# Output projection and normalisation in token chunks of 512, 512 and 128

## The reference, cut to what matters

```python
h = rmsnorm(x, norm_g) * (1.0 + scale) + shift          # scale, shift, gate: one set per group
y = merge_branches(g, (o_na, o_f, o_d), zs, w_branch[l], w_out[l])   # last step: y @ w_out
xs = xs + gate * y
...
y_sample = rmsnorm(xs, final_g)                          # after the last layer; y_prompt likewise
```

## Time and profile before

| What | Value |
|---|---|
| Time, median of 3 runs (lowest to highest) | 2940.79 us (2940.73 to 2941.08) |
| The profiled execution's own time | 2940.5 us |
| Its span, first to last instruction | 2938.6 us |
| TensorE busy | 2877.4 us, 98% of the span |
| VectorE, ScalarE, GpSimd busy | 45%, 37%, 21% |
| Matmuls of the output stage (L823) in the chain that ended last | 6% of the span |
| Granted TensorE clock, mean | 0.996 |

### The profile page before, as it was taken

How to read it: one execution, slowest core, us unless ns; L and a number is a source line. 1 busy time by engine, 2 the same in 40 slices (tenths; PEclk the granted TensorE clock), 3 DMA queues, 4 the chain that set the end, 5 groups by cost and what they waited for, 6 DMA issues and landing times.

```text
span 2938.6 us, 44082 instructions
## 1 busy us (share of the span) xinstructions
PE 2877.4 (98%) x18396; PEld 2756.4 (94%) x18396; DVE 1330.6 (45%) x2291; ACT 1076.5 (37%) x1947; POOL 614.0 (21%) x312
## 2 busy tenths in 40 slices
PE   6999999999999999999999999999999999999998
PEld 5999999999999999999999999999999989899997
DVE  4343443123557575446344434421146567554543
ACT  4333333221444544422343333323133444443231
POOL 0221221122221212122431221211221121211242
PEclk9999999999999999999999999999999999999999
DMA  5332224102111102254421121220211111215532
GB/s 224 102 110 82 102 90 137 67 15 78 42 47 47 48 32 94 80 203 141 133 79 65 66 82 39 94 83 22 70 41 45 44 48 47 78 51 183 165 110 94
DMA packets 84278, 248.55 MB, mean 85 GB/s; under 512 B 9201, under 2 KB 30193, under 8 KB 83057
## 3 DMA queue, kind: packets, MB, share of 16 engines
q1 hardware_dynamic: 84080, 245.74, 24.5%
HBM read 191.71 MB, written 54.00 MB: 84 GB/s over the span
## 4 chain that ended last, share of the span: by engine, by line
PE 89%; DVE 5%; ACT 2%; DMA 2%; issue 1%; SPq 1%; DVEq 0%; POOL 0%; POOLq 0%; ACTq 0%
PE ps L730 44%; PE ps L713 18%; PE ps L823 6%; PE ps L769 6%; PE ps L900 3%; PE ps L1041 3%; PE ps L1032 2%; PE ps L961 2%; PE ps L888 2%; PE ps L943 1%; DVE e L1839 1%; DVE stat L1822 1%; ACT e L1435 1%; DMA wmod<-w_mod 1%; DVE aTl L1846 1%
## 5 line engine op out<-in xcount | busy, mean ns | idle before, releaser
L730 PE MATMUL ps<-hhi,whi 128*128 128x384 f32 x2640 | 916.3, 347 | 5.7 <-DVE obuf L1854 3.3
L730 PE MATMUL ps<-hhi,wlo 128*128 128x384 f32 x2640 | 886.3, 336 | 0.0
L730 PE MATMUL ps<-hlo,whi 128*128 128x384 f32 x2640 | 884.1, 335 | 0.0
L1956 POOL TENSOR_TENSOR wlo<-wraw,whi 128x1024 fp32r<-128x1024 f32 (+1 forms) x188 | 415.8, 2212 | 2063.6 <-ACT whi L1127 2063.5
L730 PEld LDWEIGHTS ps<-hhi,whi 128*128 128x128 f32 x2640 | 500.0, 189 | 24.1 <-issue 7.3
L730 PEld LDWEIGHTS ps<-hlo,whi 128*128 128x128 f32 x2640 | 497.1, 188 | 0.9
L730 PEld LDWEIGHTS ps<-hhi,wlo 128*128 128x128 f32 x2640 | 495.9, 188 | 0.0
L1127 ACT ACTIVATE whi<-wraw 128x1024 fp32r<-128x1024 f32 (+1 forms) x188 | 174.5, 928 | 229.9 <-PE ps L713 209.3
L1444 ACT ACTIVATE aTh<-ps 128x512 fp32r<-128x512 f32 (+1 forms) x200 | 96.5, 482 | 278.4 <-PE ps L1032 278.4
L1691 DVE TENSOR_TENSOR ptl<-ps,pth 128x512 fp32r<-128x512 f32 (+1 forms) x144 | 82.1, 611 | 246.8 <-ACT pth L1301 246.6
L1822 DVE TENSOR_REDUCE stat<-ps 128x1 f32<-128x1152 f32 x144 | 176.5, 1231 | 16.9 <-PE ps L769 16.0
(11 more groups left out here) (199 smaller groups left out, 4835.8 us busy)
## 6 DMA issues: line engine op xcount, KB each, us to landing
wraw<-w_in SPq DMA_DIRECT2D x128, 512.0 KB, 4.2
gates_dram<-gst SPq DMA_DIRECT2D x48, 576.0 KB, 3.0
gth<-gates_dram SPq DMA_DIRECT2D x48, 576.0 KB, 4.9
mraw<-w_mod SPq DMA_DIRECT2D x32, 512.0 KB, 3.8
wraw<-w_branch SPq DMA_DIRECT2D x48, 256.0 KB, 2.8
bias<-rpb SPq DMA_DIRECT2D x8, 1280.0 KB, 6.0
outs_dram<-obuf SPq DMA_DIRECT2D x16, 576.0 KB, 3.9
oraw<-outs_dram SPq DMA_DIRECT2D x16, 576.0 KB, 3.8
```

The source lines that it names most:

```text
L730: x = mm(ps[:, bank, 0:CH], a[:, s % 2, k, :], b[:, k, n * CH:(n + 1) * CH], start=(k == 0 and a is whi and b is hhi), stop=(k == KT - 1 a ...
L1956: g_.tensor_tensor(lo[:, 0:kt, :], wraw[:, n % 2, 0:kt, :], hi[:, 0:kt, :].bitcast(F32), ALU.subtract).then_inc(S.w_lo, 1)
```

## The change

The output stage and the normalisation behind it run over chunks of 512, 512 and 128 tokens, so that the last chunk is just the context tokens and each instruction has one modulation. The two-part instructions of chunk 2 go. The buffers `xold`, `csqs` and `csq` grow to 512 columns; `crstd` and `ctn` also, and move over a part of the gate buffer `gth`, which is free then. The residual kept in DRAM and the output are split into two latent chunks and one context part. All counts of units, semaphores and the order on each engine stay. The units of the next layer's input projection keep chunks of 384.

```diff
+OC = ((0, 512), (512, TL), (TL, T))
...
-    xold = pl("xold", [P, 4, CH])
-    csqs = pl("csqs", [P, CH])
-    csq = pl("csq", [P, 2, CH])
-    crstd = pl("crstd", [P, CH])
-    ctn = pl("ctn", [P, 2, CH])
+    xold = pl("xold", [P, 4, 512])
+    csqs = pl("csqs", [P, 512])
+    csq = pl("csq", [P, 2, 512])
...
+    pl = Place(arena0 + KT * TB + 4 * KT * TILE_B)
+    crstd = pl("crstd", [P, 512])
+    ctn = pl("ctn", [P, 2, 512])
...
-    def parts(n):
-        if n < NC - 1:
-            return ((0, CH, 0),)
-        return (0, TL - n * CH, 0), (TL - n * CH, CH, 1)
+    def token_part(n):
+        return slice(OC[n][0], OC[n][1]), OC[n][1] - OC[n][0], int(n == NC - 1)
...
             def sum_squares(l, n):
                 pe.wait_ge(S.sq_added, (l * NC + n + 1) * (KT - 1))
-                mm(ps[:, 5, 0:CH], ones[:], csqs[:], start=True, stop=True).then_inc(S.ss_done, 1)
+                w = token_part(n)[1]
+                mm(ps[:, 5, 0:w], ones[:], csqs[:, 0:w], start=True, stop=True).then_inc(S.ss_done, 1)
...
-                hi, lo = halves(s)
+                (hi, lo), (cols, w, _) = halves(s), token_part(n)
...
-                        x = mm(ps[:, bank, 0:CH], a[:, k, :], b[:, k, n * CH:(n + 1) * CH],
+                        x = mm(ps[:, bank, 0:w], a[:, k, :], b[:, k, cols],
...
-                        for a, b, j in parts(n):
-                            x = v.scalar_tensor_tensor(out=xT[:, m, n * CH + a:n * CH + b], in0=ps[:, 6 + m % 2, a:b],
-                                                       scalar=mul_g[:, m, j:j + 1], in1=xold[:, i % 4, a:b],
-                                                       op0=ALU.mult, op1=ALU.add)
-                        x.then_inc(S.out_evac, 1)
+                        cols, w, j = token_part(n)
+                        v.scalar_tensor_tensor(out=xT[:, m, cols], in0=ps[:, 6 + m % 2, 0:w], scalar=mul_g[:, m, j:j + 1],
+                                               in1=xold[:, i % 4, 0:w], op0=ALU.mult, op1=ALU.add).then_inc(S.out_evac, 1)
```

More of the change, by code:

```diff
@@ L638, in old_load @@
                         sp.wait_ge(S.out_evac, l * NC * KT + i - 3)
-                    sp.dma_start(xold[:, i % 4, :], xs_dram[n, m] if l else x_in[m, :, n * CH:(n + 1) * CH]).then_inc(x_load[i % 4], 16)
+                    cols, w, ctx = token_part(n)
+                    kept = xs_ctx[m] if ctx else xs_dram[n, m]
+                    sp.dma_start(xold[:, i % 4, 0:w], kept if l else x_in[m, :, cols]).then_inc(x_load[i % 4], 16)
                 def result(n, half):
@@ L685, in _ @@
                         sp.wait_ge(S.out_evac, out_no(l, n, m) + 1)
-                        sp.dma_start(xs_dram[n].rearrange("k p t -> p k t"),
-                                     xT[:, :, n * CH:(n + 1) * CH]).then_inc(S.store, 16)
+                        cols, w, ctx = token_part(n)
+                        sp.dma_start((xs_ctx if ctx else xs_dram[n]).rearrange("k p t -> p k t"), xT[:, :, cols]).then_inc(S.store, 16)
                     if l + 1 == DEPTH and n and m in (5, KT - 1):
@@ L1209, in chunk_squares @@
                     act.wait_ge(S.sq_added, (KT - 1) * u + m - 2)
-                fn(csq[:, m % 2, :] if m else csqs[:], xT[:, m, n * CH:(n + 1) * CH], ACT.Square).then_inc(S.sq_ready, 1)
+                cols, w, _ = token_part(n)
+                fn(csq[:, m % 2, 0:w] if m else csqs[:, 0:w], xT[:, m, cols], ACT.Square).then_inc(S.sq_ready, 1)
             def chunk_norms(l, n):
@@ L1217, in chunk_norms @@
                     act.wait_ge(*((S.y_ready, n * KT) if l else (S.h_ready, KT + n * KT)))
-                fn(crstd[:], ps[:, 5, 0:CH], ACT.Ln, bias=eps[:, 0:1], scale=1.0 / D)
+                w = token_part(n)[1]
+                fn(crstd[:, 0:w], ps[:, 5, 0:w], ACT.Ln, bias=eps[:, 0:1], scale=1.0 / D)
                 act.drain()
-                fn(crstd[:], crstd[:], ACT.Exp, scale=-0.5).then_inc(S.rstd_ready, 1)
+                fn(crstd[:, 0:w], crstd[:, 0:w], ACT.Exp, scale=-0.5).then_inc(S.rstd_ready, 1)
             def chunk_high(n, m):
@@ L1559, in chunk_scaled @@
                 i = n * KT + m
[L1560 to L1563, removed]
+                cols, w, j = token_part(n)
+                v.scalar_tensor_tensor(out=ctn[:, i % 2, 0:w], in0=xT[:, m, cols], scalar=mul_a[:, m, j:j + 1],
+                                       in1=crstd[:, 0:w], op0=ALU.mult, op1=ALU.mult).then_inc(S.t_ready, 1)
             def chunk_input(n, m):
@@ L1574, in chunk_input @@
                 dve.wait_ge(S.hi_ready, KT + i + 1)
[L1575 to L1579, removed]
+                cols, w, j = token_part(n)
+                v.scalar_tensor_tensor(out=hlo[:, m, cols], in0=ctn[:, i % 2, 0:w], scalar=modr[:, m, j:j + 1],
+                                       in1=hhi[:, m, cols].bitcast(F32), op0=ALU.add, op1=ALU.subtract).then_inc(S.h_ready, 1)
             def chunk_result(n, m):
@@ L1585, in chunk_result @@
                     dve.wait_ge(S.rstd_ready, 2 + NC + n)
-                x = xT[:, m, n * CH:(n + 1) * CH]
-                v.scalar_tensor_tensor(out=x, in0=x, scalar=fgcol[:, m:m + 1], in1=crstd[:], op0=ALU.mult, op1=ALU.mult
+                cols, w, _ = token_part(n)
+                x = xT[:, m, cols]
+                v.scalar_tensor_tensor(out=x, in0=x, scalar=fgcol[:, m:m + 1], in1=crstd[:, 0:w], op0=ALU.mult, op1=ALU.mult
                                        ).then_inc(S.y_ready, 1)
@@ L1964, in add_squares @@
                 pool.wait_ge(S.sq_ready, KT + out_no(l, n, m) + 1)
-                g_.tensor_tensor(csqs[:], csqs[:], csq[:, m % 2, :], ALU.add).then_inc(S.sq_added, 1)
+                w = token_part(n)[1]
+                g_.tensor_tensor(csqs[:, 0:w], csqs[:, 0:w], csq[:, m % 2, 0:w], ALU.add).then_inc(S.sq_added, 1)
             g_.memset(ident[:], 0.0)
@@ L2136 @@
                "new_diff_v": lambda a: heads_rows(a, 1)}
-    y = np.ascontiguousarray(r["y_out"].transpose(0, 3, 1, 2).reshape(T, D))
-    return y[None, TL:], grid_rows(y[:TL]), *(as_rows[n](r[n]) for n in as_rows)
+    y = np.ascontiguousarray(r["y_out"].transpose(0, 3, 1, 2).reshape(TL, D))
+    return np.ascontiguousarray(r["y_ctx"].reshape(D, TC).T)[None], grid_rows(y), *(as_rows[n](r[n]) for n in as_rows)
```

16 lines of the change are left out of this document (9 added, 7 removed).

## The result

The changed kernel takes 2968.3 us (median of three executions: 2968.21, 2985.09, 2968.30) against 2940.79: **1.0116 times the time before, with an interval of 1.0095 to 1.0136**. The direction was forecast, the size was not: 2968.3 lies 11 us above the forecast of 2957 and 2.3 above the end of the range. The profiled execution took 2968.21 us, with a span of 2966.3 and a mean granted clock of 0.992.

The account below looks back on a forecast made before the run. TensorE, busy for 98% of the span, was taken to bound the kernel. Terms 15.9 + 3.1 + 3.7 − 1.4 − 5.0 = +16.3 us on the profiled 2940.5 gave 2956.8, 2957 against the median; range 2947 to 2966.

Parts of the forecast that it names:

- The matmuls: Output matmuls, both layers: a set of 512, 512, 128 takes 568 ns, 41.5 more than three of 384; +15.9 us.
- rival 2: 128-column matmuls run at their columns' pace, 65 ns, with weight loads hidden: 2943 us, not slower; chance 0.11.
- pairs in two halves of the array: Attention-score pairs of 512 columns, 0.2275 us a pair, taken as the pace of 512-column output matmuls: 228 ns.
- the bound by proportion, 234: 512-column output matmuls: growth proportional to columns from 175.5 ns at 384 gives 234 ns; 4.6 us more.
- The sum of squares: Last chunk's unit 0, both layers: TensorE waits 1.55 us for chunk 1's sum of squares; +3.1 us.
- The input chain: Layer 0's last chunk: making the next layer's inputs on VectorE and ScalarE outlasts the matmuls, TensorE waits; +3.7 us.
- the 2.45 us for each of the five tiles behind it: Layer 0's input chain: five tiles with an add before them take some 2.45 us each, 2.8 before.
- The forecast's lower bound: Layer 0's input chain: wait of 0 if GpSimd doesn't hold hlo, ending 27.4 us after chunk 1's last matmul starts.
- The first chunk and the end: Layer 0's first chunk covers most of its 1.66 us wait, −1.4 us; shorter work after the last matmul, −5.0 us.
- Rival 4: The clock falls in the short chunks, loads and matmuls at half pace: about 21 us a layer, 2999; chance 0.03.
- the forecast's own second term: The sum-of-squares wait at the start of the last chunk, 1.55 us in each layer; +3.1 us.

Follow-up runs that it names:

- 448, 448, 256 kernel: The changed kernel with chunks of 448, 448 and 256 in both layers instead of 512, 512 and 128: 2939.78 us, 1.0002.
- kernel with wider streams: The changed kernel with each output matmul of the last chunk streaming its 128 columns twice, the second copy unused: 2959.17 us, 1.0067.
- layer-0 kernel: Chunks of 512, 512 and 128 in layer 0's output stage only, layer 1 keeping three of 384: 2971.25 us, 1.0101.
- kernel with later inputs: The changed kernel with inputs and results of chunk 1 begun one unit later in the last chunk: four executions, 2957.82 to 2998.63 us, 1.0113.
- layer-1 kernel: Chunks of 512, 512 and 128 in layer 1 only, layer 0 keeping three of 384: 2964.39 us, 1.0086.
- late sums in layer 1: Chunk 1's sum of squares moved behind five eighths of unit 1: changed kernel 2959.13 us, with inputs also later 2956.05; layer-1 kernel 2942.5.

## Why the prediction was wrong, step by step

**The matmuls: right in kind, 2.7 us too small.** The price of 128 columns was forecast as 112 ns and is 111.5, so rival 2 (65 ns) is out. That the load of weights is this limit fits the loads 0.11 us apart in the earlier trace rows, but no run here tests it alone. The 512 columns cost 231.7 instead of 228: pairs in two halves of the array were a bad stand-in, and the bound by proportion, 234, was nearer. A set is 48.4 ns dearer, times 384: +18.6, not +15.9. The 448, 448, 256 kernel shows that this is the 128 columns' doing. The rule of the Trainium skill (TensorE: Matmul & The Clock Gate, Back-to-back issue gap) that would have made it nothing, with 81 ns at 128 columns and 131 at 512, is not what these rows show: they have 111.5 and 231.7.

**The sum of squares: right as a wait.** Forecast 1.55 us in each layer, +3.1; measured 1.3 and 1.7, together 3.0.

**The input chain: too large.** Forecast +3.7, measured 0.9, all in one wait for xT. The start was right: hlo in the changed kernel took 2.85 us beside a GpSimd weight split of 2.81. The step that failed is the 2.45 us for each of the five tiles behind it. The timeline of VectorE in the kernel with wider streams, where the clock held in the last chunks, shows tiles 2.01 us apart.

```profile
1499.85 0.34 DVE L1941 SCALAR_TENSOR_TENSOR xT<-ps,mul_g,xold 128x128 f32<-128x128 f32 x1
...
1501.18 0.75 DVE L1585 SCALAR_TENSOR_TENSOR hlo<-ctn,modr,hhi 128x512 fp32r<-128x512 f32 x1
1501.85 0.35 DVE L1941 SCALAR_TENSOR_TENSOR xT<-ps,mul_g,xold 128x128 f32<-128x128 f32 x1
...
1503.86 0.35 DVE L1941 SCALAR_TENSOR_TENSOR xT<-ps,mul_g,xold 128x128 f32<-128x128 f32 x1
```

An hlo of 512 columns is 0.75 us long here, less than the 1.03 of one of 384 in the earlier trace rows. In the kernel before, the hlo of 1.03 us run beside a GpSimd sum of squares that starts some 0.4 us ahead of them, and one that has none beside it takes 0.61; the sums of the new last chunk are narrower, 0.46 to 0.92 us:

```profile
1483.64 1.01 POOL L1965 TENSOR_TENSOR csqs<-csqs,csq 128x384 f32<-128x384 f32 x1 [1.77 <-ACT csq L1210]
```

```profile
1492.83 0.61 DVE L1576 SCALAR_TENSOR_TENSOR hlo<-ctn,modr,hhi 128x384 fp32r<-128x384 f32 x1
```

So the forecast carried a length over from a place with another neighbour; that the neighbour is the cause was not tested. The forecast's lower bound doesn't follow from its rows either: with hlo at 1.05 instead of 2.83 us the chain ends 1.8 us earlier, at T+30.6 and not T+27.4. In the wider kernel the seven tiles end 12.4 us after the first one instead of 15.6, and TensorE doesn't wait for the adds in the last chunk. In the changed kernel as measured, the fallen clock also gave VectorE time to catch up (argued, not tested alone).

**The first chunk and the end: right.** The idle time of layer 0's first chunk is 49.15 − 48.89 = 0.26 us instead of 1.66: −1.4, as forecast. The end is 10.1 us instead of 15.06, −5.0, as forecast; the eight results take 2.19 us instead of 4.32. Not in the sum: TensorE's wait of 0.9 us for a weight split in layer 1's first chunk, which the longer matmuls of that chunk cover now.

**The clock: the step that decided.** The sum put the clock at nothing. Rival 4 had the right effect and nearly the right price, 21 us a layer and 2999 us, and got 3 in 100; what starts the fall it did not say. The layer-0 kernel measures 21.0, layer 1 18.7. (An execution of the kernel with later inputs took 2998.63; that this meets the 2999 is in part luck, since that sum holds 3.7 us for an input chain that didn't come so.) The argument against the rival was that a chunk of 128 columns "keeps TensorE loading or multiplying all the time". This is the sentence that failed: TensorE is 99% busy over 40 us of the layer-1 kernel's last chunk, and the clock is 0.50 all through it. And the forecast's own second term put a wait of 1.55 us into such a stream, without asking what the clock does there.

Of the changed stages, only layer 0's lost the clock in the first profile. It cost 14.20 − 72 × 0.1115 = 6.2 us in the last chunk and 4.77 − 15 × 0.1755 = 2.1 in the next layer's first unit, 8.3 together; without them 2968.2 would have been about 2960, inside the range. So, by stages: layer 0's output stage 9.3 (half of 18.6) + 1.3 + 0.9 − 1.4 + 6.2 = 16.3, measured 16.0; layer 1's 9.3 + 1.7 − 0.9 = 10.1, measured 9.9; the end −5.0; together a measured 20.9 of the 27.7. The 6.8 outside are 3.0 from the kernel's start, 2.1 from that first unit, and some 1.7 after it. Set against each other matmul by matmul, the kernel before loses 1.6 there to a fall of the clock behind its wait for the weights of v, which the kernel after doesn't have; the kernel after loses 1.9 to a longer VectorE step in layer 1 (below) and 1.5 to a fall of the clock right behind that. At the start, nothing is changed: there the windows 20 to 40 and 40 to 60 us have a clock of 0.95 and 0.88 before and 0.83 and 0.75 after, and the other profiles here range from 0.81 to 0.96 and from 0.75 to 0.89, with nothing changed at that place either.

Where the clock holds, the time is near the forecast: 2957.82 us in the profiled kernel with later inputs, +17.3 on the 2940.5 of the profile before, where +16.3 was forecast for the changed one. But that is luck, a nearness of terms that cancel: the matmuls cost 2.7 us more, the input chain at least 2.8 less and the first chunk of layer 1 0.9 less, and 3.2 of the 17.3 lie outside the changed stages (matmul by matmul as above: 0.8 ahead of layer 0's, 2.4 between the two).

## What to carry to other kernels

Before cutting a stream of matmuls, look up the pace of its narrowest piece: here 256 columns are still on the line of columns and 128 are not, and 448, 448, 256 costs the same as three of 384. Before cutting a piece that narrow, look for every wait of TensorE ahead of it or in it, even of 1 to 2 us: in front of matmuls of 384 columns it cost its own length and at most a few us at the low clock, and in front of those of 128 it could cost the clock for the whole stream. Then judge by several executions: with one and the same kernel the time came as 2968 or as 2985 to 2992.

## What the runs showed of the hardware that was not expected

Matmuls of 128 columns with a weight load each ran at 1.2 GHz for 38 us while TensorE was 99% busy, at 213 ns each; matmuls of 384 columns had the clock back 3.5 us after a wait of 1.92 us. Streaming each matmul's columns twice made layer 1's last chunk faster, 21.05 us for 177 matmuls against 37.67. And where TensorE didn't wait in the narrow stream (the late sums in layer 1), it ran at 1.00 to its end.

A change can move a conflict in a place it doesn't touch. In layer 1's attention, VectorE and GpSimd timelines of the kernel before, then of the kernel after, and the window behind:

```profile
2350.46 1.42 DVE L1839 SCALAR_TENSOR_TENSOR e<-e,stat,e 128x1152 f32<-128x1152 f32 x1
2351.97 3.24 DVE L1803 TENSOR_TENSOR xr<-xr,sinT 128x1024 f32<-128x1024 f32 x1
...
2350.70 3.42 POOL L1956 TENSOR_TENSOR wlo<-wraw,whi 128x1024 fp32r<-128x1024 f32 x1 [20.13 <-ACT whi L1127]
```

```profile
2369.76 3.50 DVE L1843 SCALAR_TENSOR_TENSOR e<-e,stat,e 128x1152 f32<-128x1152 f32 x1
2373.34 1.23 DVE L1807 TENSOR_TENSOR xr<-xr,sinT 128x1024 f32<-128x1024 f32 x1
...
2369.64 2.39 POOL L1958 TENSOR_TENSOR wlo<-wraw,whi 128x1024 fp32r<-128x1024 f32 x1 [20.12 <-ACT whi L1132]
```

```profile
2374.00:2379.00 5.00, 5.00 (x30) 4.38 (x30) 2.62 (x3) 0.60 (x1) 0.00 (x0) 0.66 0.02 3
```

Before, the weight split starts 0.24 us after `e`, and the step behind `e`, which runs beside the split, takes 3.24 us instead of 1.23; TensorE doesn't wait for it. After, the split starts 0.12 us ahead of `e`, `e` takes 3.50 us instead of 1.42, and TensorE waits 1.72 us for that. Behind this wait the clock falls as well, for some 3 us.
